# A two-layer streaming encoder on one core, with TensorE's filler products removed

## What is computed

```
# layer 0: mLSTM mixer;  layer 1: windowed attention with sinks (mixer B), shared K/V
h = _layer_norm(DN_ALPHA * h + mix, ln_g[layer, 0], ln_b[layer, 0])
ffn = _grouped_moe(h, w_router, b_router, w_gu[layer], w_down[layer])
h = _layer_norm(DN_ALPHA * h + ffn, ln_g[layer, 1], ln_b[layer, 1])

# _grouped_moe(x, ...), 16 experts in 4 groups, 2 experts of one group for each token
probs = softmax(t @ w_router)
sel = (probs + b_router).reshape(-1, 4, 4)            # best group by its two best experts
gate = one_hot(two best experts of the best group) * w
for e in range(16):
    g, u = split(t @ w_gu[e], 2)
    out = out + gate[:, e:e + 1] * ((silu(g) * u) @ w_down[e])
```

## Time and profile before

| | before |
|---|---|
| median of three runs | 695.02 us (694.52 to 695.11) |
| the profiled execution, its own time | 691.62 us |
| its span, first to last instruction | 689.9 us |
| mean granted TensorE clock | 0.993 |
| TensorE (PE) busy | 652.9 us, 95% |
| VectorE (DVE) busy | 277.3 us, 40% |
| ScalarE (ACT) busy | 142.3 us, 21% |
| GpSimd (POOL) busy | 23.0 us, 3% |
| DMA | 231.41 MB, 335 GB/s over the span |

### The profile page before, as it was taken

The page is one execution under the profiler, slowest core; times in us unless marked ns, Lnnn a source line. Parts: engine busy times, 40 slices in busy tenths (PEclk is TensorE's granted clock), DMA queues, the critical chain, the costliest instruction groups (busy, mean ns, idle before and its releaser), DMA issues.

```text
span 689.9 us, 7089 instructions
## 1 busy us (share of the span) xinstructions
PE 652.9 (95%) x2750; PEld 289.5 (42%) x2750; DVE 277.3 (40%) x708; ACT 142.3 (21%) x325; POOL 23.0 (3%) x44
## 2 busy tenths in 40 slices
PE   5999999999999999999979998999999999999974
PEld 4864564455333333333324455555333333343321
DVE  0001203334536345353545254456253444435356
ACT  1003343122121121111222041412121121021212
POOL 2040100000000000000000011200000000000000
PEclk9999999999999999999999999999999999999998
DMA  8999905161999999999999971732899999999991
GB/s 323 388 406 407 376 1 189 55 244 66 418 420 423 420 421 422 420 422 421 420 419 412 421 323 35 332 145 99 320 423 420 423 420 420 421 420 423 420 396 64
DMA packets 39318, 231.41 MB, mean 335 GB/s; under 512 B 8041, under 2 KB 8041, under 8 KB 13682
## 3 DMA queue, kind: packets, MB, share of 16 engines
q1 hardware_dynamic: 34848, 230.70, 81.6%
q10 hardware_dynamic: 4434, 0.21, 0.5%
HBM read 229.85 MB, written 1.05 MB: 335 GB/s over the span
## 4 chain that ended last, share of the span: by engine, by line
PE 81%; DMA 9%; DVE 5%; ACT 2%; issue 1%; POOL 1%; SPq 0%; POOLq 0%; DVEq 0%; ACTq 0%
PE pb L588 28%; PE pb L410 18%; PE pb L615 14%; DMA ring<-in_w_down 8%; PE pb L448 4%; PE pb L635 3%; PE pb L742 2%; PE pb L570 2%; PE pb L381 1%; PE pb L572 1%; PE pb L536 1%; DMA h<-in_x 1%; PE pb L388 1%; PE pb L499 1%; PE pb L545 1%
## 5 line engine op out<-in xcount | busy, mean ns | idle before, releaser
L410 PE MATMUL pb<-ring,hT 128*128 128x512 f32 x320 | 141.3, 595 | 0.8 <-DVE hT L1502 0.8
L615 PE MATMUL pb<-ring,bufC 128*64 128x512 f32 x512 | 117.0, 597 | 4.9 <-DVE bufA L1336 2.7
L588 PE MATMUL pb<-ring,hT 128*64 128x512 f32 x512 | 114.4, 594 | 1.9 <-DMA ring<-in_w_gu 1.9
L588 PE MATMUL pb<-ring,bufB 128*64 128x512 f32 x512 | 113.2, 593 | 1.9 <-DVE bufC L1319 1.9
L1310 DVE STREAM_TRANSPOSE bufC<-bufC 32x128 f32<-32x128 f32 x256 | 102.9, 402 | 3.8
L1336 DVE COPY bufA<-pb 32x512 f32<-32x512 f32 x64 | 43.7, 683 | 122.9 <-PE pb L615 121.9
L410 PEld LDWEIGHTS pb<-ring,hT 128*128 128x128 f32 x320 | 59.5, 190 | 70.7 <-issue 68.7
L588 PEld LDWEIGHTS pb<-ring,hT 128*64 128x64 f32 x512 | 36.0, 137 | 74.7 <-issue 68.5
L588 PEld LDWEIGHTS pb<-ring,bufB 128*64 128x64 f32 x512 | 36.2, 137 | 73.9 <-issue 70.0
L615 PEld LDWEIGHTS pb<-ring,bufC 128*64 128x64 f32 x512 | 35.0, 136 | 72.7 <-issue 68.1
L974 ACT ACTIVATE bufA<-pb 32x512 f32<-32x512 f32 x64 | 37.7, 589 | 115.9 <-PE pb L615 115.1
(11 more groups left out here) (218 smaller groups left out, 408.7 us busy)
## 6 DMA issues: line engine op xcount, KB each, us to landing
ring<-in_w_gu SPq DMA_DIRECT2D x128, 1024.0 KB, 24.2
ring<-in_w_down SPq DMA_DIRECT2D x64, 1024.0 KB, 26.0
ring<-in_w_in_a SPq DMA_DIRECT2D x12, 1024.0 KB, 17.6
ring<-in_w_out_a SPq DMA_DIRECT2D x4, 1024.0 KB, 21.2
ring<-in_w_q_b SPq DMA_DIRECT2D x4, 1024.0 KB, 24.3
ring<-in_w_out_b SPq DMA_DIRECT2D x4, 1024.0 KB, 22.9
ring<-in_w_kv_shared SPq DMA_DIRECT2D x2, 1024.0 KB, 26.9
h<-in_x SPq DMA_DIRECT2D x4, 256.0 KB, 5.0
```

What stands on the lines that cost most here:

```text
L410: last = mm(pb[bank][:, :], hT[:, k, t * P:(t + 1) * P], slot(i0 + k // 2)[0][:, k % 2, c * HALF:(c + 1) * HALF], start=k == 0, stop=k == ...
L588: last = mm(pb[0][c * 64:(c + 1) * 64, :].rearrange("p (a n) -> p a n", a=2), xe[m % 2][:, k, g * SLOTS:(g + 1) * SLOTS], slot(u_gu(l, u) ...
L615: last = mm(pb[2][c * 64:(c + 1) * 64, :], heT[u == EXPERTS - 1][:, (2 * hf + j) * 64:(2 * hf + j + 1) * 64], w[:, j, c * HALF:(c + 1) * H ...
```

## The change

All calls of `stay_awake` are taken out, and the function with them. No other instruction is added, moved or altered, on any engine; 14 products (28 instructions of TensorE, each with its weight load) are gone. Line numbers behind the function fall by 5 to 9.

```diff
-            def stay_awake(bank, n):
-
-                for _ in range(n):
-                    mm(pb[bank][:, :], ident[:, :], ident[:, 0:1].to_broadcast([P, HALF]), start=True, stop=True)
-
...
             def moe(l):
                 for t in range(NT):
                     if t:
-                        stay_awake(1, 3)
                         turn_h(2 + 2 * l, 2 * l, t, 0)
...
                     for c in range(2):
                         mm(pb[4 + 2 * t + c][:, :], alpha_i[:, :], h[:, t, c * HALF:(c + 1) * HALF],
                            start=True, stop=False, skip_group_check=True)
-                stay_awake(3, 1)
                 pe.wait_ge(chosen, l + 1)
...
-                stay_awake(3, 1)
                 for f, bank in enumerate((1, 3, 2, 1)):
                     gather(0, f, bank)
                 gate_up(0)
...
             moe(0)
-            stay_awake(0, 4)
             turn_h(3, 1, 0, 4)
```

## The result

The changed kernel takes 700.95 us (median of 4 runs, 699.46 to 701.35) against 694.77 us before in the same session (694.51 to 695.11): a ratio of 1.0091, 95% interval 1.0075 to 1.0106, 6.2 us slower. 700.8 us was forecast. In what follows, a fall is a stretch in which the granted clock is 0.50 (1.2 GHz); wide work is products of 512 columns on all 128 rows, thin work is products of few columns or few rows, or waits.

A forecast was written before the change was run, and what follows sets the result against it. Each layer was taken to end a fixed time after its first expert product; 1.62 + 2.48 + 1.70 = 5.8 us on the profiled 691.62 gave 697.4, plus 3.4 to the median: 700.8 us, range 697.6 to 704.8.

The forecast's parts named there:

- three places: Clock falls forecast at second router rows of layer 0, those of layer 1, and between experts and mixer B.
- Direct gains: Time saved by removing fillers: 0.7 to 0.86 us behind layer 0's alpha products, nothing elsewhere.
- Transposes at half clock, +0.5 us: Ahead of the second router rows: the last four of eight transposes run at half clock, 0.5 us more per layer.
- Second router rows doubled, 1.81 to 3.62 us: In both layers the clock falls before or at their start, so 1.81 us become 3.62 us.
- Alpha products as in layer 0 before, 5.38 us: In both layers these dense products bring the clock back, taking layer 0's earlier 5.38 us.
- The sum for the places: Start of L551, behind the alpha products: 1.62 us later in layer 0, 2.48 us later in layer 1.
- Between experts and mixer B, +1.70 us: K/V products start at 1.2 GHz and bring the clock back: 1.70 us more, bounds 0 and 3.7 us.
- The layers end a fixed time behind their first expert product: In both layers, delay of the first expert product delays transfer restart and layer end one for one.
- The 3.4 us between the profiled execution and the median: Whole kernel: timed median 695.02 us against 691.62 us profiled, a difference added unchanged to the forecast.
- Late fall: Rival: clock falls only inside the alpha products and ahead of L742, +1.2 us, 696.2 us; chance 0.10.
- The clock holds: Rival: no fall, fillers only delayed L551 behind late alpha products; 1.7 us faster, 693.3 us; chance 0.05.
- long fall: Rival: place products and gathers run slow too, up to 4 us in a layer, 705 us and above; chance 0.13.

The follow-up runs named there:

- e2: Kernel before without the filler behind the alpha products, in both layers: 693.66 us against 694.83, ratio 0.998.
- e4: Kernel before without the four fillers ahead of mixer B: 695.87 us against 694.83, ratio 1.0014.
- e12: The changed kernel, run once more on the chip of the other runs: 702.20 us against 694.62 for the kernel before, ratio 1.0107.
- e3: Kernel before without the filler ahead of the gathers, in both layers: 694.60 us against 694.83, ratio 1.000.
- e7: Kernel before, fillers kept, with narrow work in the mLSTM mixer split by useful dense work: 692.64 us against 694.14, ratio 0.9973.
- e6: Kernel before with every filler product kept at 512 columns but filling only 4 of 128 rows: 707.43 us, ratio 1.0218.
- e8: As e7, with one alpha product moved between the transposes and the second router rows in each layer: 692.39 us against 694.14 for the kernel before, ratio 0.9987.
- e10: As e7, with the four 4-row broadcasts parted two by two by dense products: 690.46 us against 694.62 for the kernel before, ratio 0.9938.
- e9: Kernel before with only the six fillers between the router rows kept, the other eight dropped: 696.85 us against 694.62, ratio 1.0031.

## Why the prediction was right, and where not

The time was right (700.8 forecast, 700.95 measured), and so was the mechanism, with its three places. That the two numbers agree to 0.15 us is luck: one term was 0.8 us too small, and the measured difference is between kernels whose usual executions differ from the profile that the sum starts from.

- *Direct gains.* None between the router rows, ahead of the gathers and ahead of mixer B: shown, with L876 late next, as said (9.20 us from scatter to K/V product in both). Behind the alpha products 0.7 to 0.86 us where these are late: e2 shows it, 0.76 us in layer 0.
- *Transposes at half clock, +0.5 us:* from the first to the second router rows 6.44 us became 6.82 in layer 0 and 7.01 in layer 1, +0.38 and +0.57.
- *Second router rows doubled, 1.81 to 3.62 us:* measured from their start to that of the alpha products 3.43 us in both layers, +1.62 in place of +1.81.
- *Alpha products as in layer 0 before, 5.38 us:* from their start to L544 5.98 and 5.35 us. The 5.38 us are the time until the last product ends; from start to start it was 5.21 us (e2, 153.95 to 159.16). The same slip is in the bound of a late fall, 0.17 us later in layer 1, which e2 shows as nothing. And the "sixteen products of only 16 columns" ahead of the fall in layer 0 are sixteen instructions, eight products.
- *The sum for the places,* +1.62 and +2.48 us: measured +1.92 and +2.23 us to the first expert product, 4.15 us in place of 4.10.
- *Between experts and mixer B, +1.70 us:* this term was sized too low. It is +2.54 us in the profile (3.70 to 6.24), 2.15 in e4, 2.73 in e12. The clock fell at 372.7 us, after the transposes and just ahead of the K/V products. The stretch at 0.50 lasted to 379.5 us, so 5.1 us of it lay in these products, more than the 3.4 us that the alpha products had in layer 0 before (155.1 to 158.5 us). The premise that did not hold is that dense products end such a stretch after 3 to 4 us: in the changed kernel it went on for about 5 us of the alpha products in layer 0, 3.7 us in layer 1, and 5.1 us of the K/V products.
- *The layers end a fixed time behind their first expert product:* right for the restart of the transfers, only roughly for the end: +0.50 us in layer 0's stretch and -1.09 us in layer 1's, with code and transfers the same. Over the kernels from first expert product of layer 1 to the end of the span it is 205.9 to 207.4 us, without an order that follows the edits. What makes this difference is open; it is the size of what stays open in e4.
- *The 3.4 us between the profiled execution and the median,* "for reasons that the trace does not show": by the profiles of the kernels with the same code and the clocks of the timed runs they are for the most part two more falls in the mLSTM mixer, in most executions, that the profile of before had missed. Carrying the difference over unchanged was right by luck: the same two falls are in the changed kernel, and that was not known. The thin rows L473 and L493 would have let one suspect them. If most executions of before also have a late fall in layer 1, as the profiles of e3 and e7 do and that of e4 does not, the change costs 1.48 us there (21.77 - 20.29) in place of 2.23, and the places add up to 5.9 us, near the 6.2 measured, in place of 6.7; no profile of before shows that.
- *Late fall* as a rival was priced with 0.17 us in layer 1 and a gain of 0.69 us in layer 0; e2 shows the gain (0.76 us) where the clock falls late. As what the change would bring it is out: the clock fell ahead of the second router rows. *The clock holds* is out. The *long fall* into the gathers did not come in the changed kernel, but in e6 (5.33 us of gathers) and e8.

## What to carry to other kernels

A filler on an engine with a clock that follows its work was paid back here where it stands in a wait that would be there anyway, and where it is as wide and as full as real work: those with few columns or few rows only added delay. Before adding fillers, look for narrow work that stands in a row (one-column sums, few-row broadcasts) and put it between products that have to be done anyway; that gave 0.6% here (e10), on top of the fillers, and adds no work. And look at several executions before taking one profile's clock for the kernel's: of the ten profiles here of kernels with the same code up to 146 us, eight show the two early falls and two do not.

## What the runs showed of the hardware that I had not expected

- Filled rows matter to the granted clock: behind six instructions of 512 columns on 4 rows it fell ahead of the second router rows (e6, 3.59 us), behind six on 128 rows it did not (1.96 us in before, e3, e4 and e9).
- A fall inside the alpha products costs nothing (e2, 3.3 us at half clock), a fall ahead of the second router rows about 2 us a layer (+1.92 and +2.23; 10.1 us at half clock), ahead of the K/V products 2.10 to 2.73 us (6.7 to 6.8 us at half clock): the price of a fall is how long it lasts and the chain that it hits.
- Executions of one kernel spread with their mean granted clock: the kernel before took 690.3 to 697.2 us over the runs of this study, e10, whose profile has no fall, 689.83 to 691.24 us.
